# A six-layer fp32r transformer kernel on one core: joined matmuls of two widths, a mask in place of bias matmuls, and a reordered attention pipeline

## The chip, the cores and the metric

The kernel runs on one core of one Trainium2 chip. Its time is device microseconds (us) of that core for one execution; lower is better. The engines are PE (TensorE, matmuls), DVE (VectorE), ACT (ScalarE), POOL (GpSimd) and SP (SyncE, which issues DMA transfers). Each engine runs its own list of instructions in order, and the lists meet through semaphores.

## The reference

256 tokens of width 1024 in fp32 pass through two blocks. The first is a token mixer (8 heads of forgetting attention, 8 heads of banded attention) and a convolutional feed-forward layer; the second is a layer of retention with latent attention (MLA) and a layer of block-sparse attention (MoBA, 16 heads). Each ends in a residual and a layer norm. What matters here:

```python
def forgetting_attention(q, k, v, log_f):
    cum = jnp.cumsum(log_f.astype(jnp.float32), axis=-1)
    ...
        logits = jnp.einsum('bhqd,bhkd->bhqk', qb, k).astype(jnp.float32) * scale
        logits = logits + cb[..., :, None] - cum[..., None, :]
        ...
        logits = jnp.where(causal, logits, -jnp.inf)
        p = jax.nn.softmax(logits, axis=-1)

def conv_ffn(x, w_up, conv_w, conv_b, w_down):
    u = x @ w_up
    ...
    u = sum(u_pad[:, j:j + s, :] * conv_w[j] for j in range(CONV_WIDTH)) + conv_b
    value, gate = jnp.split(u, 2, axis=-1)
    return (value * jax.nn.gelu(gate)) @ w_down
```

## The kernel before

**Projections.** Every operand of a projection is held as two parts, hi and lo (hi is the value rounded to the fp32r type, lo the rest), and a product is the sum of three matmuls, hi by hi, hi by lo and lo by hi (`three`, lines 821 to 825). Weights arrive in 236 pieces of 128x1024 (512 KB each) in a buffer `raw`; ACT writes `w_hi` (`split_hi`, L1117) and DVE writes `w_lo` (`split_lo`, L1283) into a ring of six. Projections are cut into chunks (`chunks`); a chunk has a kind, a number of pieces and a place in four PSUM banks (`acc` 0 to 3). Kind F makes two tiles of 128 features by 256 tokens side by side in one bank: the weights stand still and the tokens move, 256 columns a matmul, 8 steps of the inner dimension. The feed-forward layer's up projection is 22 such pairs of tiles (value and gate). Two of them (`up01`) are made otherwise; `up2` to `up21` are kind F, one bank each.

**Convolution.** After the last matmul of `up j`, ACT makes the middle tap (`taps`, L1125) from PSUM, DVE adds the other two (`convolve`, L1326, four instructions), ACT makes the gelu, POOL multiplies, and ACT and DVE split the result (`h_split`, L1233 and L1447).

**Attention.** Heads go in pairs, `firsts` in `attention` being the first of each. Steps of a pair: `scores` on PE (L940, and for forgetting heads a second set, L949, four rows deep, that adds the cumulated gates through `cumA` and `cumB`); `soft` on DVE (adds the mask, takes the maximum, writes the probabilities' buffer `pr`); `exp` on ACT; `norm` on DVE; `pt` on PE (three 128x128 transposes a head, L959); a copy to `ptb` on ACT; `pv` on PE (the value products, L979); `yout` and `ylo`, which leave the result as hi and lo parts. Scores use job banks 0 and 1, transposes 2 and 3, value products 3 (banks 4 to 7 of `acc`). Layer one has 8 pairs (4 forgetting, 4 banded), layer two 4, layer three 8.

**Order.** `plan` writes one list of steps, `ORDER`, from which every engine takes its own. `run` emits a chunk's matmuls in halves of a piece; after each half, groups of attention steps from `pending` are emitted at a given rate (`background`), and splits run four pieces ahead. So an attention step sits on PE between projection matmuls. The last projection of each layer (`out1`, `down`, `out2`, `out3`, kind B) is normed by `norm_first`, `norm_half` and `norm_last`.

## Time and profile before

| | |
|---|---|
| median of 3 runs | 767.89 us (767.82 to 768.12) |
| the profiled execution | 768.47 us, of which the span from first to last instruction is 766.7 |
| mean granted TensorE clock | 0.996 of full speed |
| PE busy | 752.5 us, 98% |
| PE weight loads busy | 659.6 us, 86% |
| DVE busy | 528.8 us, 69% |
| ACT busy | 382.5 us, 50% |
| POOL busy | 36.8 us, 5% |
| DMA | 130.62 MB, mean 170 GB/s |

Matmuls are pipelined: one of 256 columns shows a duration of 0.28 us and the next starts 0.12 us after it. What a matmul takes of PE is the distance from its start to the next start, and that is how PE's rows are read here. For DVE and ACT the distance between starts is likewise a little less than the duration shown.

### The profile page before, as it was taken

The page shows a single profiled execution, that of the slowest core. Times are in us where ns is not written, and L with a number is a line of the kernel's source. Part 1 is how long each engine was busy: PE and PEld are TensorE (multiplying, and loading weights), DVE is VectorE, ACT ScalarE, POOL GpSimd, SP SyncE. Part 2 cuts the span into 40 slices and gives each one's busy share as a digit, 9 for nine tenths or more (in the row PEclk, how much of TensorE's full clock was granted, in tenths as well). Part 3 has the DMA queues.
Part 4 walks back from the last instruction along what each step waited for, and adds up shares of the span by engine and source line. Part 5 has one row for each costly group of instructions (what it writes and reads, how often), then busy time and mean ns, then how long its engine had stood idle before and what let it go on. Part 6 is the DMA issues. An engine that isn't in the chain of part 4 may idle for free.

```text
span 766.7 us, 12680 instructions
## 1 busy us (share of the span) xinstructions
PE 752.5 (98%) x4838; PEld 659.6 (86%) x4838; DVE 528.8 (69%) x940; ACT 382.5 (50%) x629; POOL 36.8 (5%) x50
## 2 busy tenths in 40 slices
PE   8999999999999999999999999999999999999995
PEld 8897777899999988799899777987788879988964
DVE  4654758697788854857686566965574587977766
ACT  5655763575655654156554444433443434565450
POOL 0000000021111200100000000000000010000001
PEclk9999999999999999999999999999999999999998
DMA  8852345456655685265536334553576617446402
GB/s 304 316 192 89 114 155 199 165 162 190 188 183 165 212 295 194 69 221 192 165 109 196 126 133 138 161 185 129 185 264 200 221 52 233 136 133 196 162 2 82
DMA packets 37580, 130.62 MB, mean 170 GB/s; under 512 B 4304, under 2 KB 4688, under 8 KB 37392
## 3 DMA queue, kind: packets, MB, share of 16 engines
q1 hardware_dynamic: 36144, 125.09, 49.2%
q0 software_dynamic: 1232, 4.46, 1.9%
q8 instruction: 39, 0.64, 0.3%
q10 hardware_dynamic: 144, 0.26, 0.1%
q14 instruction: 21, 0.17, 0.1%
HBM read 128.74 MB, written 1.05 MB: 169 GB/s over the span
## 4 chain that ended last, share of the span: by engine, by line
PE 95%; DVE 3%; issue 1%; DMA 1%; ACT 0%; DVEq 0%; SPq 0%
PE acc L823 28%; PE acc L825 27%; PE acc L824 27%; PE acc L940 2%; PE acc L959 2%; PE acc L979 2%; PE acc L998 1%; PE acc L938 1%; PE acc L1011 1%; PE acc L946 1%; DMA res<-in_x 1%; PE acc L972 0%; PE acc L1022 0%; PE acc L1037 0%; PE acc L1035 0%
## 5 line engine op out<-in xcount | busy, mean ns | idle before, releaser
L1283 DVE TENSOR_TENSOR w_lo<-raw,w_hi 128x1024 fp32r<-128x1024 f32 (+1 forms) x223 | 260.8, 1197 | 70.1 <-ACT w_hi L1117 69.3
L1117 ACT ACTIVATE w_hi<-raw 128x1024 fp32r<-128x1024 f32 (+1 forms) x223 | 224.4, 1034 | 88.8 <-PE acc L825 77.6
L823 PE MATMUL acc<-X_hi,w_hi 128*128 128x256 f32 x848 | 243.0, 287 | 0.6 <-DVE w_lo L1558 0.6
L824 PE MATMUL acc<-X_lo,w_hi 128*128 128x256 f32 x848 | 239.8, 283 | 0.0
L825 PE MATMUL acc<-X_hi,w_lo 128*128 128x256 f32 x848 | 239.8, 283 | 0.0
L823 PEld LDWEIGHTS acc<-X_hi,w_hi 128*128 128x128 f32 x848 | 162.5, 192 | 6.3 <-issue 5.1
L824 PEld LDWEIGHTS acc<-X_lo,w_hi 128*128 128x128 f32 x848 | 162.6, 192 | 0.5 <-issue 0.2
L825 PEld LDWEIGHTS acc<-X_hi,w_lo 128*128 128x128 f32 x848 | 162.5, 192 | 0.0
L823 PE MATMUL acc<-w_hi,S_hi 128*128 128x512 f32 x256 | 101.7, 397 | 1.3 <-DVE gate L1346 1.3
L824 PE MATMUL acc<-w_lo,S_hi 128*128 128x512 f32 x256 | 99.8, 390 | 0.0
L825 PE MATMUL acc<-w_hi,S_lo 128*128 128x512 f32 x256 | 99.7, 390 | 0.0
L823 PE MATMUL acc<-w_hi,X_hi 128*128 128x512 f32 (+1 forms) x192 | 74.4, 388 | 0.9 <-DVE w_lo L1283 0.9
L825 PE MATMUL acc<-w_hi,X_lo 128*128 128x512 f32 (+1 forms) x192 | 71.6, 373 | 0.0
L824 PE MATMUL acc<-w_lo,X_hi 128*128 128x512 f32 (+1 forms) x192 | 71.4, 372 | 0.0
L823 PEld LDWEIGHTS acc<-w_hi,S_hi 128*128 128x128 f32 x256 | 48.1, 188 | 13.0 <-issue 1.8
L825 PEld LDWEIGHTS acc<-w_hi,S_lo 128*128 128x128 f32 x256 | 48.1, 188 | 10.1
L824 PEld LDWEIGHTS acc<-w_lo,S_hi 128*128 128x128 f32 x256 | 48.1, 188 | 9.6 <-issue 0.2
L1326 DVE SCALAR_TENSOR_TENSOR v<-acc,cvp,v 128x255 f32<-128x255 f32 (+1 forms) x88 | 38.3, 477 | 20.9 <-ACT v L1125 20.1
L823 PEld LDWEIGHTS acc<-w_hi,X_hi 128*128 128x128 f32 x192 | 36.2, 189 | 9.4 <-issue 3.9
L1125 ACT ACTIVATE v<-acc,cvp 128x256 f32<-128x256 f32 x44 | 22.3, 561 | 42.6 <-PE acc L825 38.4
L825 PEld LDWEIGHTS acc<-w_hi,X_lo 128*128 128x128 f32 x192 | 36.2, 188 | 6.6
L824 PEld LDWEIGHTS acc<-w_lo,X_hi 128*128 128x128 f32 x192 | 36.3, 189 | 6.0 <-issue 0.5
(165 smaller groups left out, 795.7 us busy)
## 6 DMA issues: line engine op xcount, KB each, us to landing
raw<-in_w SPq DMA_DIRECT2D x225, 512.0 KB, 4.3
raw<-in_w SPq DMA_DIRECT2D x11, 256.0 KB, 3.1
gate<-in_ln_gain POOLq DMA_DIRECT2D x4, 512.0 KB, 5.2
gate<-in_ln_bias POOLq DMA_DIRECT2D x4, 512.0 KB, 5.7
res<-in_x SPq DMA_DIRECT2D x4, 256.0 KB, 4.2
gate<-in_bias SPq DMA_DIRECT2D x1, 1024.0 KB, 10.3
out<-res SPq DMA_DIRECT2D x4, 256.0 KB, 2.0
decay<-in_decay SPq DMA_DIRECT2D x1, 512.0 KB, 6.1
```

What stands on the lines that cost most here:

```text
L823: nc.tensor.matmul(out, a_hi, b_hi, start=start, stop=False)
L824: nc.tensor.matmul(out, a_hi, b_lo, start=False, stop=False)
L825: return nc.tensor.matmul(out, a_lo, b_hi, start=False, stop=stop)
L938: nc.tensor.matmul(dst, qT[s][:, h, q], kT[s][:, h, 0:nk], start=True, stop=False)
L940: last[i] = nc.tensor.matmul(dst, qT[s][rows, h // 2, q], kT[s][rows, h // 2, 0:nk], start=True, stop=kind != "fox")
L946: last[i] = nc.tensor.matmul(dst, qpeT[rows, h // 2, q], kpeT[rows, 0, 0:nk], start=False, stop=True)
L959: last = nc.tensor.transpose(job[:, 2 + j % 2, b * P:(b + 1) * P], pr[:, j % 2, b * P:(b + 1) * P], ident)
L979: last = nc.tensor.matmul(job[i * HD:(i + 1) * HD, 3, q0:q0 + n], vv[s][:, tt, v], ptb[:, (j + i) % 2, b0:b0 + n], start=tt == 0, stop=tt ...
L1117: nc.scalar.activation(home(u, "hi")[:, 0:n], raw[:, u % RAW, 0:n], ACT.Copy).then_inc(hi_done, 1)
L1125: return [nc.scalar.activation(conv[j % 2][:, i, :], up[:, i * S:(i + 1) * S], ACT.Identity, scale=cvp[:, 2, i, j:j + 1], bias=cvp[:, 3, i ...
L1283: nc.vector.tensor_tensor(home(u, "lo")[:, 0:n], raw[:, u % RAW, 0:n], home(u, "hi")[:, 0:n].bitcast(F32), ALU.subtract).then_inc(lo_done, 1)
L1326: last = nc.vector.scalar_tensor_tensor(o, up[:, i * S:i * S + S - lag], cvp[:, 2 - lag, i, j:j + 1], o, ALU.mult, ALU.add)
```

## The change

Six things are changed together.

1. `up2` to `up21` become kind W. The tokens' hi and lo parts now lie side by side (`X`, 512 columns for each step of the inner dimension), and one matmul of 512 columns with `w_hi` takes the place of two of 256; one of 256 with `w_lo` stays. A tile then fills a whole bank, its second half holding what comes of the lo part, and a chunk takes two banks. ACT copies the two second halves to `rtmp` and DVE adds the first halves to them; taps and convolution read `rtmp` and are put into the next chunk.
2. Forgetting heads: the matmuls of L949 are gone. POOL writes the cumulated gates (8 rows of 256) to DRAM and reads them back for all partitions; DVE adds the causal mask once (`fox_mask`), and `soft` adds the head's tile in place of the causal constant. (The term that belongs to the query falls out of the softmax.) DVE's work on the gates leaves `evac` of `f` and becomes the step `forgotten`, three halves later.
3. `attention` for layers one and three: `pv` of a pair stands directly behind the scores of the pair after the next, and `pt` stands alone in the middle of the round. For that a second set of probabilities (`spare`) lies where MLA's rotary parts lie, and `pr` and `spare` take turns.
4. `out3` starts in banks 2 and 3 instead of 0 and 1, and takes both its first pieces' first token tiles before their second.
5. The second half of the first weight piece is loaded after two of four pieces of `x`, and split after two of the four transposes.
6. The buffers for all this (`X`, `peT`).

```diff
@@ chunks @@
-        add(f"up{j}", "F", 2, "X", k8, "dve", ("conv", j),
+        add(f"up{j}", "W", 2, "X", k8, "dve", ("conv", j),
...
-    add("out3", "B", 8, "S", k8, "dve", ("norm", 3), ("w_out_odd", k8, None))
+    add("out3", "B", 8, "S", k8, "dve", ("norm", 3), ("w_out_odd", k8, None), at=2)
@@ plan @@
+        if of != "L2":
+            for i, e in enumerate(firsts):
+                p, o = (firsts[i - 1] if i else None), (firsts[i - 2] if i > 1 else None)
+                s0, s1, s2, s3 = [("scores", e)], [("exp", e), ("soft", e + 1)], [("exp", e + 1), ("norm", e)], [("norm", e + 1)]
+                if o is not None:
+                    s0.append(("pv", o))
+                    s1 = [("yout", o)] + s1 + ([("ylo", o)] if of == "L1" else [])
+                    s3 += [("ylo", o)] if of == "L3" else []
+                if p is not None:
+                    s2 += [("pt", p), ("pt", p + 1)]
+                s0.append(("soft", e))
...
+                pending.extend(zip(need, (s0, s1, s2, s3), gives))
+            o, p = firsts[-2:]
+            pending.append(({JOBS[o]["v"]}, [("pv", o), ("pt", p)], set()))
+            pending.append((gates(o), [("yout", o), ("ylo", o), ("pt", p + 1)], done(o)))
+            pending.append(({JOBS[p]["v"]}, [("pv", p)], set()))
+            pending.append((gates(p), [("yout", p)], set()))
+            pending.append((set(), [("ylo", p)], done(p)))
+            return
...
-    split_to(1)
+        if i == 1:
+            split_to(1)
...
-        run(name, 0)
+        run(name, 0, inside={(1, 1): [("forgotten",)]} if name == "kA0" else {})
...
-            run(f"up{j}", 0, tail=first if j == 2 else ())
+            run(f"up{j}", 0, tail=first if j == 2 else (),
+                inside={(0, 1): [("taps", j - 1)], (1, 0): [("conv", j - 1)]} if j > 2 else {})
...
-    run("out3", 1, lambda i: {f"L3y{i}"})
+    run("out3", 1, lambda i: {f"L3y{i}"}, early=2)
@@ PE @@
+                elif kind == "W":
+                    wait_operand(step, ch, [("X", tt, part) for tt in range(NT)])
+                    for k in range(4 * part, 4 * part + 4):
+                        w = slice(k * P, (k + 1) * P)
+                        nc.tensor.matmul(acc[:, b0 + i, :], wh[:, w], X[:, k, :, :], start=k == 0, stop=False)
+                        last = nc.tensor.matmul(acc[:, b0 + i, 0:S], wl[:, w], X_hi[:, k, :], start=False, stop=k == KT - 1)
...
-                        elif kind == "fox":
-                            r = slice(cum_row(h), cum_row(h) + 4)
-                            last[i] = nc.tensor.matmul(dst, cumA[r, h // 4, q], cumB[r, h // 4, 0:nk], start=False, stop=True)
@@ ACT @@
-                    last = taps(j, acc[:, b0, :])[1]
-                    last.then_inc(tap_act, 1)
+                    if j >= 4:
+                        act.wait_ge(conv_done, j - 1)
+                    nc.scalar.activation(rtmp[:, j % 2, :].rearrange("p (i s) -> p i s", i=2), acc[:, b0:b0 + 2, S:2 * S], ACT.Copy)\
+                        .then_inc(half_copied, 1)
...
+            def up_taps(j):
+                act.wait_ge(evac_dve, CH[BY[f"up{j}"]]["count"])
+                taps(j, rtmp[:, j % 2, :])[1].then_inc(tap_act, 1)
@@ DVE @@
-                    for g in range(2):
-                        for o, name in ((cumA, "cumA"), (cumB, "cumB")):
-                            k = const(name)
-                            last = nc.vector.tensor_scalar(o[:, g, :], fox[:, 0, :], k[:, g:g + 1], k[:, 2 + g:3 + g],
-                                                           ALU.mult, ALU.add)
-                    last.then_inc(evac_dve, 1)
+                    nc.vector.tensor_scalar(fox[:, 0, :], acc[:, b0, 0:S], bforget, None, ALU.add).then_inc(evac_dve, 1)
                 elif kind == "conv":
-                    convolve(e[1], acc[:, b0, :]).then_inc(evac_dve, 1)
+                    both = rtmp[:, e[1] % 2, :].rearrange("p (i s) -> p i s", i=2)
+                    dve.wait_ge(half_copied, e[1] - 1)
+                    nc.vector.tensor_tensor(both, both, acc[:, b0:b0 + 2, 0:S], ALU.add).then_inc(evac_dve, 1)
...
+            def fox_mask():
+
+                dve.wait_ge(cum_out, 16 * 2)
+                dve.wait_ge(const_in, 16)
+                tri = const("causal")[:, 0:P].unsqueeze(1).to_broadcast([P, 4, P])
+                for i in range(2):
+                    nc.vector.tensor_tensor(corner[:, 4 * i:4 * i + 4, :], forgot[i][:, :, 0:P], tri, ALU.add)
+                    last = nc.vector.tensor_tensor(forgot[i][:, :, P:S], forgot[i][:, :, P:S], tri, ALU.add)
+                link(last)
...
-                if j >= 2:
+                if jb["kind"] == "mla" or j in (24, 25):
                     dve.wait_ge(pt_ready, j - 1)
+                elif j >= 4:
+                    dve.wait_ge(pt_ready, j - 3)
+                x = probs(j)
...
+                elif jb["kind"] == "fox":
+                    first, rest = corner[:, jb["h"], :], forgot[jb["h"] // 4][:, jb["h"] % 4, :]
@@ POOL @@
+                    elif e[0] == "forget":
+                        pool.wait_ge(cum_ready, 1)
+                        pool.dma_start(cum_dram, fox[0:8, 2, :]).then_inc(cum_done, 16)
+                        pool.wait_ge(cum_done, 16)
+                        for i in range(2):
+                            pool.dma_start(forgot[i], cum_dram[4 * i:4 * i + 4, :].partition_broadcast(P)).then_inc(cum_out, 16)
@@ SP @@
+                        if (tt, q) == (0, 1):
+                            sp.dma_start(raw[:, 0, 512:1024], t["w"][0, :, 512:1024]).then_inc(landed[0], 16)
```

How instructions move, at three places. First PE in layer one, around the scores of the third pair of heads (forgetting heads 4 and 5). Before, L959 are the transposes of the second pair, L940 and L949 the scores of the third, L979 the value products of the second:

```order
380 L959 MATMUL acc<-cst,pr 128x128 x6
381 L940 MATMUL acc<-kT,qT 128x128 x2
382 L949 MATMUL acc<-rot 128x128 x2
383 L940 MATMUL acc<-kT,qT 128x256 x2
384 L949 MATMUL acc<-rot 128x256 x2
385 L979 MATMUL acc<-ptb,v 64x256 x2
386 L979 MATMUL acc<-ptb,v 64x128 x2
```

In the changed kernel L979 are scores, L1015 value products, L995 transposes:

```order
374 L979 MATMUL acc<-kT,qT 128x128 x2
375 L979 MATMUL acc<-kT,qT 128x256 x2
376 L1015 MATMUL acc<-ptb,v 64x256 x2
377 L1015 MATMUL acc<-ptb,v 64x128 x2
...
384 L995 MATMUL acc<-cst,peT 128x128 x6
```

The four-row matmuls are gone, the value products (now of the first pair) follow the scores, and the transposes (of the second pair, read from the spare set) come after the next projection matmuls. In this pair value products followed the scores before too; in the others projection matmuls stood between.

Then PE in the up projection, where one step of the inner dimension is three rows before and two in the changed kernel:

```order
708 L823 MATMUL acc<-X_hi,w_hi 128x256
709 L824 MATMUL acc<-X_lo,w_hi 128x256
710 L825 MATMUL acc<-X_hi,w_lo 128x256
```

```order
701 L908 MATMUL acc<-X,w_hi 128x512
702 L909 MATMUL acc<-X,w_lo 128x256
```

And DVE in the same stage, one chunk before (L1326 is the convolution, L1447 the split of `h`, L1283 the weight splits):

```order
184 L1326 SCALAR_TENSOR_TENSOR v<-acc,cvp,v 128x255 x2
185 L1326 SCALAR_TENSOR_TENSOR v<-acc,cvp,v 128x254 x2
186 L1447 TENSOR_TENSOR S_lo<-v,S_hi 128x256
187 L1283 TENSOR_TENSOR w_lo<-raw,w_hi 128x1024 x2
```

and one chunk of the changed kernel:

```order
191 L1418 TENSOR_TENSOR rtmp<-rtmp,acc 128x512
192 L1504 TENSOR_TENSOR S_lo<-v,S_hi 128x256
193 L1325 TENSOR_TENSOR w_lo<-raw,w_hi 128x1024
194 L1368 SCALAR_TENSOR_TENSOR v<-rtmp,cvp,v 128x255 x2
195 L1368 SCALAR_TENSOR_TENSOR v<-rtmp,cvp,v 128x254 x2
196 L1325 TENSOR_TENSOR w_lo<-raw,w_hi 128x1024
```

DVE has one instruction more, the convolution is that of the chunk before, and it stands between the two weight splits.

## Rows read from the trace of the kernel before

**Rows 1.** The page: busy time, share of the span, instructions.

```profile
PE 752.5 (98%) x4838; PEld 659.6 (86%) x4838; DVE 528.8 (69%) x940; ACT 382.5 (50%) x629; POOL 36.8 (5%) x50
```

**Rows 2.** Timeline of PE, up projection: start, duration, instruction.

```profile
240.06 0.28 PE L823 MATMUL acc<-X_hi,w_hi 128*128 128x256 f32 x1
...
240.42 0.28 PE L823 MATMUL acc<-X_hi,w_hi 128*128 128x256 f32 x1
```

**Rows 3.** Timeline of PE, down projection, matmuls of 512 columns.

```profile
300.00 0.39 PE L823 MATMUL acc<-w_hi,S_hi 128*128 128x512 f32 x1
...
300.68 0.39 PE L823 MATMUL acc<-w_hi,S_hi 128*128 128x512 f32 x1
```

**Rows 4.** Timeline of PE, the first pair's scores (forgetting heads).

```profile
48.74 0.49 PE L940 MATMUL acc<-kT,qT 64*128 64x128 f32 x4
...
50.22 0.70 PE L949 MATMUL acc<-rot 4*128 4x256 f32 x4
50.85 0.39 PE L823 MATMUL acc<-X_hi,w_hi 128*128 128x256 f32 x1
```

**Rows 5.** Timeline of PE, the first scores of layer three.

```profile
651.30 0.93 PE L940 MATMUL acc<-kT,qT 64*128 64x128 f32 x8
652.16 0.38 PE L823 MATMUL acc<-X_hi,w_hi 128*128 128x256 f32 x1
```

**Rows 6.** Timeline of PE: transposes of three pairs in layer one.

```profile
55.27 1.18 PE L959 MATMUL acc<-cst,pr 128*128 128x128 f32 x6
...
65.32 0.82 PE L959 MATMUL acc<-cst,pr 128*128 128x128 f32 x6
...
73.23 1.06 PE L959 MATMUL acc<-cst,pr 128*128 128x128 f32 x6
```

**Rows 7.** Timeline of PE: scores and value products without, then with matmuls between.

```profile
67.54 0.70 PE L949 MATMUL acc<-rot 4*128 4x256 f32 x4
68.17 0.87 PE L979 MATMUL acc<-ptb,v 128*64 128x256 f32 x8
...
83.20 0.50 PE L823 MATMUL acc<-w_hi,X_hi 128*128 128x512 f32 x1
83.54 0.40 PE L824 MATMUL acc<-w_lo,X_hi 128*128 128x512 f32 x1
...
84.48 0.39 PE L825 MATMUL acc<-w_hi,X_lo 128*128 128x512 f32 x1
84.80 0.87 PE L979 MATMUL acc<-ptb,v 128*64 128x256 f32 x8
```

**Rows 8.** Timeline of PE at the start: idle time and its releaser in brackets.

```profile
10.58 0.39 PE L823 MATMUL acc<-X_hi,w_hi 128*128 128x256 f32 x1 [0.59 <-DVE w_lo L1558]
24.74 0.47 PE L823 MATMUL acc<-w_hi,X_hi 128*128 128x512 f32 x1 [0.94 <-DVE w_lo L1283]
```

**Rows 9.** Timeline of DVE at the start, the last step of the gates.

```profile
21.97 1.38 DVE L1383 TENSOR_SCALAR rot<-rtmp,cst 128x256 f32<-128x256 f32 x4
```

**Rows 10.** Timeline of PE, the first matmul of `out3`.

```profile
730.07 0.50 PE L823 MATMUL acc<-w_hi,S_hi 128*128 128x512 f32 x1 [1.33 <-DVE gate L1346]
```

**Rows 11.** Timeline of DVE, one chunk of the up projection.

```profile
203.51 1.78 DVE L1326 SCALAR_TENSOR_TENSOR v<-acc,cvp,v 128x255 f32<-128x255 f32 x4 [1.37 <-ACT v L1125]
205.21 0.41 DVE L1447 TENSOR_TENSOR S_lo<-v,S_hi 128x256 fp32r<-128x256 f32 x1
...
209.27 1.78 DVE L1326 SCALAR_TENSOR_TENSOR v<-acc,cvp,v 128x255 f32<-128x255 f32 x4 [1.38 <-ACT v L1125]
```

**Rows 12.** Groups by line and shape, whole span: busy us, mean ns.

```profile
L1311 DVE TENSOR_TENSOR qT<-acc,tab 128x512 f32<-128x512 f32 x8 | 5.4, 678 | 0.0
...
L1366 DVE SCALAR_TENSOR_TENSOR rot<-rot,small,pr 128x256 f32<-128x256 f32 x4 | 1.7, 478 | 1.1 <-POOL small L1605 1.1
```

**Rows 13.** The same view of ACT.

```profile
L1156 ACT ACTIVATE kT<-acc 128x512 f32<-128x512 f32 x3 | 1.8, 591 | 6.1 <-PE acc L825 6.1
```

**Rows 14.** DMA issues by line: size and median us to landing.

```profile
gate<-in_ln_gain POOLq DMA_DIRECT2D x4, 512.0 KB, 5.2
```

More of the change, by code:

```diff
@@ L376, in attention @@
                 steps[3].append(("ylo", p))
-            of = "" if p is None else "L1" if p < 16 else "L2" if p < 24 else "L3"
-            gives = set() if p is None else {f"{of}y{JOBS[x]['tile']}" for x in (p, p + 1)}
+            gives = set() if p is None else done(p)
             for k in range(4):
@@ L749, in place, with probs @@
             return job[:, TJ[n]["bank"], :]
+        def probs(j):
+            return spare[:, j % 2, :] if JOBS[j]["kind"] != "mla" and j // 2 % 2 else pr[:, j % 2, :]
         def bank_free(eng, step):
@@ L1254, in _ @@
                     yout(step[1])
+                elif step[0] == "taps":
+                    up_taps(step[1])
                 elif step[0] == "gelu":
@@ L1565, in _ @@
                     evac(step[1])
+                elif step[0] == "forgotten":
+                    forgotten()
                 elif step[0] == "bias":
+                    fox_mask()
                     rel_bias()
```

106 lines of the change are left out of this document (54 added, 52 removed).

## The prediction

> **What bounds the kernel now.** I read the page first: PE is busy for 98% of the span [rows 1], at a mean granted clock of 0.996. So time is gained only where PE has fewer or shorter steps, or where it waits. A matmul's duration hides its neighbours, so I then read PE's timeline by distances between starts. In the up projection three matmuls of 256 columns take 240.42 - 240.06 = 0.36 us, 0.120 each [rows 2]; in the down projection three of 512 take 0.68, 0.2267 each [rows 3]. The difference, 0.1067 us for 256 more columns, is the columns' own time, and either kind carries 0.0133 us beyond it. Last I looked for every place where the distance is longer. The waits are few: 0.59 and 0.94 us at the start [rows 8] and 1.33 before `out3` [rows 10]; the rest is the short interludes of attention between projection matmuls.
>
> **The change, part by part.**
>
> *Joined matmuls.* One step of the inner dimension goes from 3 x 0.120 = 0.360 to 0.2267 + 0.120 = 0.3467 us [rows 2, 3]. There are 8 steps in each of 2 tiles of 20 chunks, 320: 320 x 0.0133 = 4.3 us. That assumes that DVE and ACT keep up with a chunk that takes PE 16 x 0.3467 = 5.55 us instead of 5.76. DVE's cycle is 5.76 us, of which it idles 1.38, so it works 4.38 [rows 11]. It gets the addition of 512 elements from PSUM; the nearest row is 678 ns [rows 12], of which some 0.08 overlaps the next instruction, as with the convolution (1.78 us long, but 1.70 to the next start [rows 11]). So 4.38 + 0.60 = 4.98, 0.57 below 5.55. The convolution now reads SBUF; an operation of that kind with all operands in SBUF has 478 ns [rows 12], and four of it in 1.78 us [rows 11] are 0.44 apart, so I price the move at nothing. ACT gets a copy of 512 (591 ns [rows 13]) and is half busy [rows 1]. Order matters too: DVE's addition waits for ACT's copy, which waits for the chunk's last matmul, but what is queued behind it (the split of `h`, a weight split) is not wanted by PE for four pieces, that is two chunks or 11 us. The two banks of a chunk are wanted again when the next chunk ends, 5.5 us later; the copy and the addition need about 0.6 + 0.7 us plus the semaphores. Only at the first chunks, where DVE is behind with the tiles of `up01`, do I see the margin shrink, to less than 1 us, and I take off 0.3 us for it (bounds 0 and 1).
>
> The Trainium skill, page "TensorE: Matmul & The Clock Gate", section "Back-to-back issue gap", gives a gap of N/2.4 plus 2.5 ns to a warm matmul. By it one matmul fewer would save 2.5 ns, and this part would give 320 x 2.5 ns = 0.8 us in place of 4.3. The trace disagrees with it at both widths (120 and 226.7 ns against 109 and 216), and I go by the trace.
>
> *Forgetting heads.* The first pair's scores, alone between projection matmuls, take 50.85 - 48.74 = 2.11 us [rows 4]; a pair without the four-row matmuls takes 0.86 [rows 5]. Four pairs: 4 x 1.25 = 5.0 us. That is more than those matmuls' columns, since switching between the two kinds goes too. DVE's addition of the mask costs the same with a head's tile as with the constant. `fox_mask` adds four operations of 512 on DVE, about 2.4 us by the 0.60 above, ahead of the first scores, where DVE has finished its splits; if all of it came late it would push the first scores' chain by 2.4 us, which two halves of projection matmuls cover. The gates travel by DRAM: a write and two reads of 512 KB, on a queue where a transfer of that size lands in 5.2 us [rows 14]. The gates are ready at about 24 (21.97 + 1.38 before [rows 9]); with 3 us for the write, 1 to issue and 8 to land among the weights' transfers they are back at 36. The masks are wanted some 4 us ahead of the first scores (48.74 [rows 4]), at about 44. Cost nothing; each us beyond 44 would cost one.
>
> *Transposes.* In the second and fourth pairs PE's transposes take 1.18 and 1.06 us against 0.82 in the third [rows 6], because they come before the probabilities of the second head are done. They now come two halves later in the chain: 0.36 + 0.24 = 0.6 us.
>
> *Seams.* The first projection matmul after scores is followed at 83.54 - 83.20 = 0.34 us, 0.11 more than 0.227, and the value products start 84.80 - 84.48 = 0.32 after the last matmul, 0.09 more [rows 7]. Leaving fp32 and entering it again costs 0.20. Where value products directly follow scores, the distance is 68.17 - 67.54 = 0.63 [rows 7], the same as from the last scores to a projection matmul, 50.85 - 50.22 [rows 4], so the 0.20 is not paid. The new order has this seam in the third to eighth pair of both layers, 12 times, and it was there once before: 11 x 0.20 = 2.2 us. Between transposes and scores there was no such saving to lose: both are priced here by their own rows. Bounds: 0 (if taking the transposes out adds a switch) and 3.
>
> *Gates on DVE.* PE waits 0.94 us at 24.74 for a weight split [rows 8] that stands behind DVE's work on the gates, of which the last part alone is 1.38 us long [rows 9]. Now that split stands ahead of it: 0.9 us, and the four small operations become one.
>
> *`out3`.* Its first matmul waits 1.33 us for the gate of `mgt11` [rows 10], which holds bank 1. From banks 2 and 3 on, held by chunks long done, it can start, and bank 1 comes two pieces later, 2.7 us of matmuls (12 x 0.2267): 1.3 us. At the end of layer three the last pair's value products get one group of six matmuls as cover (1.4 us) instead of three; behind them lie three operations of 256 elements (0.41 each [rows 11]), about 1.3 with semaphores. I price that at nothing, bounds 0 and 0.5.
>
> *Start.* The second half of the first weights is loaded and split earlier; it can take at most the 0.59 us of [rows 8], and the last two pieces of `x` are 256 KB later. I take 0.3 (bounds 0 and 0.6).
>
> **Sum.** 4.3 - 0.3 + 5.0 + 0.6 + 2.2 + 0.9 + 1.3 + 0.3 = 14.3 us. The profiled execution took 768.47 us, 1.77 of it outside the span of 766.7; that frame stays, so it would be 754.2. The median of the runs shown is 0.58 below the profiled one, so I forecast 767.89 - 14.3 = 753.6 us. What ends the kernel, DVE's norm after `out3`, hangs on PE's matmuls of that chunk and moves with them.
>
> **The rivals.**
>
> *The joined matmuls give nothing.* Either the 0.0133 us goes with the columns read and not with the instruction, or DVE, with 0.57 us to spare, does not fit its waits in. For it: 90% load on an engine in strict order, and the `angles` operations come on top in four chunks. Against it: the same 0.0133 at two widths [rows 2, 3], and work four pieces ahead. The time is 753.6 + 4.0 = 757.6. The page's figure stands here as well, as a cost per instruction that is mostly not saved, at 757.1. Chance 0.13, of it 0.04 for the page's rule.
>
> *The attention part gives only the bias matmuls.* Seams and transposes give nothing (2.8 us), or the new order brings waits of that size: `pt` of the second head and `pv` share bank 3, and DVE carries the masks late. Against it: the distances in [rows 7]. Time 755.6 to 757. Chance 0.14.
>
> *Slower: DVE sets the pace of the up projection.* If waits for ACT's copy and taps cannot be filled with splits, a chunk lasts 4.98 us and the waits. PE then waits for banks, because a chunk has two banks of four where it had one. Each 0.1 us over 5.55 costs 20 x 0.1 = 2 us; the kernel is slower from 5.55 + 14.3 / 20 = 6.27 us on, which needs 1.3 us of unfilled waits per chunk. At 6.5 the time would be 753.6 + 19 = 772.6. Against it: a split stands between the addition and the convolution, just where a wait for the taps would be. Chance 0.05, of it 0.02 within 0.2% and 0.03 slower.
>
> *More than forecast.* The start gives all of 0.6, other seams (value products before transposes at the layers' ends) count, nothing is lost at the first chunks: below 751.8. Chance 0.04.
>
> **How the numbers follow.** The forecast case, 751.8 to 755.5, has 0.64. With the attention rival it is 0.78; taking in most of the first rival gives 751.6 to 757.7. Faster by over 0.2% (1.5 us, about what a measurement of this kernel tells from no change) holds all cases but the slower one: 0.95; within it 0.02; slower 0.03.
>
> **What would show it.** In the up projection PE's starts should be 0.227 and 0.120 us apart in turn and a chunk 5.55 us, with DVE idle about half a us per chunk; a longer chunk with an idle time released by the addition says the first or third rival. Scores and value products together should take about 0.86 + 0.80 us in every pair, with no idle time released by DVE at the transposes, and the waits at 10.6, 24.7 and at `out3` should be gone or short. A wait of DVE for the DMA that brings the gates back would be a cost I put at nothing.

## The result, and the profile after

The changed kernel takes 759.13 us in the median of 4 runs (756.82 to 759.28), the kernel before on the same chip 767.86 (767.68 to 768.12): a ratio of 0.988, 95% interval 0.986 to 0.990. That is 8.7 us or 1.1% less, where 14.3 us were forecast; the median lies above the range. The profiled execution is the fastest of the four, 756.82 us with a span of 755.0, and it is 11.65 us shorter than the profiled one of before. The miss of 5.5 us has three parts: 14.3 - 11.65 = 2.65 us that are in the trace, 2.3 us by which the median exceeds the traced run (the three others are at 759.06 to 759.28, their mean granted clock is 0.994, its own 0.996), and 0.6 because before it was the other way round and the traced run was slower than the median.

The page of the changed kernel, part 1 and two groups of part 5 (what stood at L823 to L825 is L858 to L860 now; the joined matmuls are L908 and L909):

```profile
span 755.0 us, 12053 instructions
PE 741.0 (98%) x4486; PEld 638.5 (85%) x4486; DVE 544.6 (72%) x961; ACT 394.1 (52%) x649; POOL 41.6 (6%) x53
...
L908 PE MATMUL acc<-X,w_hi 128*128 128x512 f32 x320 | 111.2, 392 | 0.0
...
L909 PE MATMUL acc<-X,w_lo 128*128 128x256 f32 x320 | 89.6, 280 | 0.0
```

PE is still busy for 98% of the span, so the gain has to be found in distances between starts again. In the up projection PE's timeline (start, duration) reads:

```profile
240.30 0.39 PE L908 MATMUL acc<-X,w_hi 128*128 128x512 f32 x1
240.53 0.28 PE L909 MATMUL acc<-X,w_lo 128*128 128x256 f32 x1
240.65 0.39 PE L908 MATMUL acc<-X,w_hi 128*128 128x512 f32 x1
```

A step of the inner dimension is 0.35 us, where it was 0.36 [rows 2]. DVE's timeline has one whole chunk from split to split:

```profile
202.83 1.23 DVE L1325 TENSOR_TENSOR w_lo<-raw,w_hi 128x1024 fp32r<-128x1024 f32 x1 [0.19 <-ACT w_hi L1153]
203.97 1.79 DVE L1368 SCALAR_TENSOR_TENSOR v<-rtmp,cvp,v 128x255 f32<-128x255 f32 x4
205.67 1.22 DVE L1325 TENSOR_TENSOR w_lo<-raw,w_hi 128x1024 fp32r<-128x1024 f32 x1
206.89 0.69 DVE L1418 TENSOR_TENSOR rtmp<-rtmp,acc 128x512 f32<-128x512 f32 x1
207.49 0.70 DVE L1504 TENSOR_TENSOR S_lo<-v,S_hi 128x256 fp32r<-128x256 f32 x1
208.38 1.23 DVE L1325 TENSOR_TENSOR w_lo<-raw,w_hi 128x1024 fp32r<-128x1024 f32 x1 [0.18 <-ACT w_hi L1153]
```

The cycle is 208.38 - 202.83 = 5.55 us, PE's pace. The addition takes 0.60 to the next start and the convolution 1.70, both as priced. DVE is shown idle for only 0.18 us of it, less than the half us foreseen. Part of the rest is the split of `h` (L1504): it takes 0.70 us in the seven chunks where POOL's multiplication runs beside it for 0.42 us, as here (POOL's starts at 207.17 and takes 0.74), and 0.42 in the chunks where the two hardly overlap; before the change the two did not meet in these chunks. From 155 to 180 us, where DVE catches up, a chunk takes it 4.91 us with no idle time, near the 4.98 of the estimate. PE never waits for DVE here.

The waits at the start of the second half (10.58), at 24.74 [rows 8] and before `out3` [rows 10] are gone. Behind the first 6 us, PE's timeline marks only these two waits:

```profile
7.66 0.55 PE L1034 MATMUL acc<-cst,res 128*128 128x128 f32 x3 [0.50 <-DMA res<-in_x]
...
108.54 0.52 PE L995 MATMUL acc<-cst,peT 128*128 128x128 f32 x3 [1.92 <-DVE S_lo L1499]
```

**By stage.** From PE's timeline I take the starts of the first projection matmul, of the first scores, of the transposes of `x` between the layers, and of the last matmul. The feed-forward layer and layer three are counted from the last of the transposes ahead of them, layer one and layer two up to the first; the two stretches of 9.0 us left out between them are the same before and after. All stages are us.

| stage | before | after | gain | forecast |
|---|---|---|---|---|
| to the first half's first projection matmul | 8.33 | 8.95 | -0.62 | start 0.3 and gates 0.9, to the first scores |
| from there to the first scores | 40.41 | 38.72 | 1.69 | |
| layer one's attention, from the first scores | 80.17 | 75.88 | 4.29 | 5.0 + 0.6 + 5 seams 1.0 |
| feed-forward layer | 180.49 | 176.59 | 3.90 | 4.3 - 0.3 |
| layer two | 299.22 | 299.28 | -0.06 | 0 |
| layer three, to the last matmul | 130.72 | 128.24 | 2.48 | 6 seams 1.2, `out3` 1.3 |

The feed-forward layer and layer three came out as forecast. Layer one gives 2.3 us less. The place is the wait at 108.54: the transposes of head 15, the last of the layer, wait 1.92 us for DVE's L1499, which is `ylo` of the pair before (heads 12 and 13). PE, ACT and DVE around it:

```profile
104.69 0.55 PE L995 MATMUL acc<-cst,peT 128*128 128x128 f32 x3
...
106.23 0.39 PE L860 MATMUL acc<-w_hi,S_lo 128*128 128x512 f32 x1
108.54 0.52 PE L995 MATMUL acc<-cst,peT 128*128 128x128 f32 x3 [1.92 <-DVE S_lo L1499]
...
105.28 0.49 ACT L1252 ACTIVATE ptb<-acc 128x384 f32<-128x384 f32 x1 [2.11 <-PE acc L995]
105.66 2.00 ACT L1153 ACTIVATE w_hi<-raw 128x1024 fp32r<-128x1024 f32 x2
107.56 0.38 ACT L1261 ACTIVATE S_hi<-acc 128x256 fp32r<-128x256 f32 x1
...
106.75 1.23 DVE L1325 TENSOR_TENSOR w_lo<-raw,w_hi 128x1024 fp32r<-128x1024 f32 x1 [2.71 <-ACT w_hi L1153]
107.97 0.42 DVE L1499 TENSOR_TENSOR S_lo<-acc,S_hi 128x256 fp32r<-128x256 f32 x1
```

Read from the end: L1499 (107.97) waits for L1261, which is `yout` (107.56). That one needs only the value products of 103.89, done by 104.8. But on ACT it stands behind two weight splits (2.00 us), and on DVE L1499 stands behind two `w_lo` splits, of which the second waits for ACT. The list of steps that `plan` writes for the changed kernel has there:

```
pv 12
pt 14
mm out1.2 p(0,)
split_hi 31
split_hi 32
split_lo 30
split_lo 31
yout 12
ylo 12
pt 15
```

`pt 15` writes bank 3. `pv 12` has left its result there, and it is free only after `ylo 12`. A second, smaller case of the same is the third pair's transposes (start 70.29), which add 0.99 us between projection matmuls where the others add 0.66.

### The profile page after: what moved, and what is told of

It is laid out like the page before. It is cut to its first block, busy times and chain, and to the rows that moved or that the text cites. A ratio compares the mean times of both kernels' runs of the same rounds, so it can differ in the third digit from the quotient of the medians.

```text
span 755.0 us, 12053 instructions
## 1 busy us (share of the span) xinstructions
PE 741.0 (98%) x4486; PEld 638.5 (85%) x4486; DVE 544.6 (72%) x961; ACT 394.1 (52%) x649; POOL 41.6 (6%) x53
## 4 chain that ended last, share of the span: by engine, by line
PE 97%; DVE 1%; DMA 1%; issue 0%; SPq 0%; DVEq 0%; ACT 0%; ACTq 0%
PE acc L858 24%; PE acc L860 23%; PE acc L859 23%; PE acc L908 10%; PE acc L909 5%; PE acc L995 2%; PE acc L979 2%; PE acc L1015 2%; PE acc L1034 1%; PE acc L977 1%; PE acc L1047 1%; DMA res<-in_x 1%; PE acc L985 1%; PE acc L1008 0%; PE acc L1058 0%; PE acc L1071 0%
## 5 line engine op out<-in xcount | busy, mean ns | idle before, releaser
L858 PE MATMUL acc<-X,w_hi 128*128 128x256 f32 x528 | 152.2, 288 | 0.1
L860 PE MATMUL acc<-X,w_lo 128*128 128x256 f32 x528 | 149.3, 283 | 0.0
L859 PE MATMUL acc<-X,w_hi 128*128 128x256 f32 x528 | 149.3, 283 | 0.0
L908 PE MATMUL acc<-X,w_hi 128*128 128x512 f32 x320 | 111.2, 392 | 0.0
L858 PEld LDWEIGHTS acc<-X,w_hi 128*128 128x128 f32 x528 | 101.1, 191 | 3.7 <-issue 3.0
L858 PE MATMUL acc<-w_hi,S_hi 128*128 128x512 f32 x256 | 101.9, 398 | 0.0
L859 PEld LDWEIGHTS acc<-X,w_hi 128*128 128x128 f32 x528 | 101.2, 192 | 0.4 <-issue 0.2
L860 PEld LDWEIGHTS acc<-X,w_lo 128*128 128x128 f32 x528 | 101.1, 192 | 0.0
L860 PE MATMUL acc<-w_hi,S_lo 128*128 128x512 f32 x256 | 99.8, 390 | 0.0
L909 PE MATMUL acc<-X,w_lo 128*128 128x256 f32 x320 | 89.6, 280 | 0.0
L858 PE MATMUL acc<-w_hi,X 128*128 128x512 f32 (+1 forms) x192 | 74.2, 386 | 0.0
L860 PE MATMUL acc<-w_hi,X 128*128 128x512 f32 (+1 forms) x192 | 71.6, 373 | 0.0
L859 PE MATMUL acc<-w_lo,X 128*128 128x512 f32 (+1 forms) x192 | 71.5, 372 | 0.0
L908 PEld LDWEIGHTS acc<-X,w_hi 128*128 128x128 f32 x320 | 59.9, 187 | 13.2
L909 PEld LDWEIGHTS acc<-X,w_lo 128*128 128x128 f32 x320 | 60.5, 189 | 0.0
L858 PEld LDWEIGHTS acc<-w_hi,S_hi 128*128 128x128 f32 x256 | 48.1, 188 | 11.1 <-issue 1.4
L860 PEld LDWEIGHTS acc<-w_hi,S_lo 128*128 128x128 f32 x256 | 48.1, 188 | 10.1
L858 PEld LDWEIGHTS acc<-w_hi,X 128*128 128x128 f32 x192 | 36.2, 189 | 7.3 <-issue 1.8
```

Of the source, the lines that this page charges most:

```text
L858: nc.tensor.matmul(out, a_hi, b_hi, start=start, stop=False)
L859: nc.tensor.matmul(out, a_hi, b_lo, start=False, stop=False)
L860: return nc.tensor.matmul(out, a_lo, b_hi, start=False, stop=stop)
L908: nc.tensor.matmul(acc[:, b0 + i, :], wh[:, w], X[:, k, :, :], start=k == 0, stop=False)
L909: last = nc.tensor.matmul(acc[:, b0 + i, 0:S], wl[:, w], X_hi[:, k, :], start=False, stop=k == KT - 1)
```

## The experiments

Theory A: bank 3 costs about 2 us at the layer's end because two weight splits stand ahead of `yout` and `ylo`, and an idle PE of about 2 us is what lets the clock fall in some runs, which is the rest. Theory B, the rival: the joined matmuls or the new order give less than priced in most runs, and the wait is only where it shows. The medians of before beside which the following were timed are 768.14 us (first four), 768.19 (next four) and 768.02 (last three). In line numbers of other kernels the same lines stand a few lines further down.

**1. `yout` and `ylo` ahead of the splits.**

```diff
-            pending.append(({JOBS[o]["v"]}, [("pv", o), ("pt", p)], set()))
-            pending.append((gates(o), [("yout", o), ("ylo", o), ("pt", p + 1)], done(o)))
+            if of == "L1":
+                pending.append(({JOBS[o]["v"]}, [("pv", o), ("pt", p), ("yout", o), ("ylo", o)], done(o)))
+                pending.append((set(), [("pt", p + 1)], set()))
...
```

> The changed kernel, but at the end of layer one the last pair but one gets its yout and ylo steps directly behind its value products, ahead of the weight splits, instead of behind them. Theory A (the second head's transposes wait at 108.5 us for bank 3, because ylo stands behind two weight splits on ACT, and the 2 us of idle PE also let the clock fall in most runs): the profiled span falls by 2.0 us to about 753.0, and the times of all runs lie together at about 754.8, 4.3 below the changed kernel's median of 759.1. Rival B (the wait is real, but the two levels of the runs come from the changed start of the kernel): the span falls by 2.0 and the times stay on two levels, about 754.8 and 757.2. Rival C (the wait only hides another one behind it, such as the copy of the probabilities): the span falls by less than 0.5.

Measured: 755.76 us (ratio 0.984, 0.983 to 0.985; one disturbed run of 4174 us is left out). Layer one's attention takes 73.99 us in the place of 75.88. PE's timeline at the place:

```profile
106.90 0.39 PE L864 MATMUL acc<-w_hi,S_lo 128*128 128x512 f32 x1
107.32 0.52 PE L999 MATMUL acc<-cst,peT 128*128 128x128 f32 x3
107.60 0.48 PE L862 MATMUL acc<-w_hi,S_hi 128*128 128x512 f32 x1
```

The wait is gone but for some 0.2 us: these transposes add 0.56 us between projection matmuls, where those at the end of layer three add 0.34. All four runs have a clock of 0.996 or 0.997. The profiled span is 753.9 us and not the 753.0 expected, because the first scores start at 48.37 us in this trace and at 47.67 in that of after. The median is 3.4 us under the first comparison's 759.13, and 2.0 under that of experiment 8, the same kernel on this chip: 1.6 under its runs at a clock of 0.997, and 3.2 under its run at 0.994. So the wait itself and something that goes with the clock are both gone.

**2. The wait filled.** The wait stays as long as it is, but PE does four matmuls of 256 columns in it (fp32, no part of the output; the trace records each as two).

```diff
             def pt(step):
                 j = step[1]
+                if j == 15:
+                    pe.wait_ge(max_done, 16)
+                    for _ in range(4):
+                        nc.tensor.matmul(job[:, 0, 0:256], kT[0][:, 0, 0:P], kT[0][:, 0, :], start=True, stop=True)
```

> The changed kernel with four more matmuls of 256 columns in fp32 on PE ahead of the transposes of head 15, so that PE works through most of the 1.9 us that it idles there; they write a bank that nothing reads. Theory A (the idle time lets the clock fall in most runs): the span stays at about 755.0 (up to 0.3 more), and all runs take about 756.8, with the mean clock 0.996. Rival B (the start decides): most runs stay at 759.1 with clock 0.994.

Measured: 757.61 us (757.08 to 757.80; 0.986, 0.985 to 0.988), the clock 0.997 in all four. The trace:

```profile
107.25 1.89 PE L995 MATMUL acc<-kT 128*128 128x256 f32 x8
109.33 0.52 PE L999 MATMUL acc<-cst,peT 128*128 128x128 f32 x3 [0.18 <-DVE S_lo L1503]
```

Layer one takes 75.85 us, the same as after, since the order of the splits is the same. (The median is 0.8 us above the 756.8 expected, and so is the start of the first scores above that of after, 48.49 to 47.67.) So the time of the wait is kept and only the idleness taken away, and the runs at the lower clock are gone with it: the four agree with the runs at 0.997 of experiment 8 (757.36 and 757.42).

**3. The old order of attention,** with all the rest of the change: `if of != "L2":` becomes `if False:`.

> The changed kernel with attention's old order in layers one and three (transposes ahead of the scores, value products a half later), the mask, the joined matmuls, out3 and the start kept. My account of the reorder (11 seams at 0.20 us gained, 2.1 us lost at head 15's transposes and 0.3 at those of the third pair): the span is about 755.0 - 2.4 + 2.2 = 754.8, and by theory A all runs lie near 756.6 on one level. If the seams gain nothing, the span is 752.6. By rival B the runs lie on two levels, most near 759.

Measured: 758.25 us (758.11 to 758.56; 0.987, 0.986 to 0.989). That is 0.5 us above the changed kernel in experiment 8 and 0.9 below it in the first comparison: the new order had little more than paid for its own wait. (By stage the trace of after is 0.6 us longer in layer one and 1.4 shorter in layer three. I had expected the old order 0.2 us shorter in all; it is 0.8 longer.) Against experiment 1, which has the new order without the wait, it is 2.5 us slower. By stage that is 75.27 - 73.99 = 1.28 us in layer one and 129.65 - 128.24 = 1.41 in layer three, 2.7 together. The forecast for the order was 2.2 for seams and 0.6 for transposes.

**4. The up projection as before,** narrow matmuls, one bank a chunk, taps and convolution from PSUM (of the edit, the part that says it).

```diff
-        add(f"up{j}", "W", 2, "X", k8, "dve", ("conv", j),
+        add(f"up{j}", "F", 2, "X", k8, "dve", ("conv", j),
...
-            run(f"up{j}", 0, tail=first if j == 2 else (),
-                inside={(0, 1): [("taps", j - 1)], (1, 0): [("conv", j - 1)]} if j > 2 else {})
+            run(f"up{j}", 0, tail=first if j == 2 else ())
```

> The changed kernel with the up projection as before: kind F, one bank a chunk, three matmuls of 256 columns a step, taps and convolution from PSUM. Forecast 320 x 0.0133 us less what the first chunks lose: the stage from the layer's first transposes to those of the next layer takes 3.9 to 4.3 us longer, the span 758.9 to 759.3. If the addition on DVE had slowed the stage, less than that.

Measured: 761.74 us (761.16 to 763.15; 0.992, 0.991 to 0.994). The feed-forward layer takes 180.49 us again, to the hundredth what it took before, and no other stage moves; the joined matmuls are worth 3.90 us there. Between the medians of experiments 4 and 8 lie 4.0 us. Its starts are 0.120 apart as in [rows 2].

**5. The bias matmuls back.** The four-row matmuls are put back in the forgetting heads' scores, adding zeros, while DVE's way of adding the gates stays.

```diff
                             last[i] = nc.tensor.matmul(dst, qT[s][rows, h // 2, q], kT[s][rows, h // 2, 0:nk],
-                                                       start=True, stop=True)
+                                                       start=True, stop=kind != "fox")
...
+                        elif kind == "fox":
+                            pe.wait_ge(const_in, 16)
+                            r = slice(64 * (h % 2) + 32 * (h // 2 % 2), 64 * (h % 2) + 32 * (h // 2 % 2) + 4)
+                            zero, mask = const("causal")[:, P:2 * P], const("causal")[:, P:3 * P]
+                            last[i] = nc.tensor.matmul(dst, zero[r, :], mask[r, 0:nk], start=False, stop=True)
```

> The changed kernel with the four-row matmuls put back behind the scores of the forgetting heads; they add zeros, so the result is that of the mask. My term: 4 x 1.25 = 5.0 us more in layer one, of which the waits of the transposes can take some away. If switching between kinds does not count, only the matmuls' own 4 x 1.05 = 4.2.

Measured: 762.85 us (762.16 to 764.88; 0.994, 0.993 to 0.995). Layer one's attention takes 80.90 - 75.88 = 5.02 us more; the forecast was 4 x 1.25 = 5.0. The other stages stay.

**6. The start as before,** on top of experiment 1.

```diff
-        if i == 1:
-            split_to(1)
+    split_to(1)
...
                     for tt, q in ((0, 0), (1, 0), (0, 1), (1, 1)):
-                        if (tt, q) == (0, 1):
-                            sp.dma_start(raw[:, 0, 512:1024], t["w"][0, :, 512:1024]).then_inc(landed[0], 16)
...
+                    sp.dma_start(raw[:, 0, 512:1024], t["w"][0, :, 512:1024]).then_inc(landed[0], 16)
```

> The kernel of e1_early_yout (changed, with the two steps ahead of the splits) with the start as before: the second half of the first weights loaded after all of x and split after the four transposes. I had given the new start 0.3 us; the traces so far show the second half of the first chunk at 10.7 to 11.1 us against 10.6 before. Theory now: the new start gives nothing, the last pieces of x come later, and this kernel is 0 to 0.4 us faster than e1_early_yout. Rival: it is 0.3 us slower.

Measured: 755.00 us (754.71 to 755.87; 0.983, 0.982 to 0.985), 0.8 us under experiment 1. The two traces, experiment 6 first:

```profile
7.21 0.66 PE L1036 MATMUL acc<-cst,res 128*128 128x128 f32 x4 [0.35 <-DMA res<-in_x]
...
8.49 0.36 PE L860 MATMUL acc<-X,w_hi 128*128 128x256 f32 x1
...
10.75 0.39 PE L860 MATMUL acc<-X,w_hi 128*128 128x256 f32 x1 [0.58 <-DVE w_lo L1617]
```

The wait of 0.58 us for the weight split is back, and the kernel is no slower, by its median faster. With the changed start the wait for the third piece of `x` is 1.14 us in experiment 1, 1.29 in experiment 8 and 0.50 in the first trace, and the first projection matmul starts at 8.95 to 9.77 us in the eight traces that have it, against 8.10 to 8.49 in those with the old start, but for experiment 11 (9.07). The first scores come 0.58 us earlier than in experiment 1. I had allowed 0 to 0.4 us; by this pair of kernels the change of the start loses 0.6 (traces) to 0.8 us (medians). How large the loss is, the runs do not settle: the first scores start at 47.67 to 48.50 us in the eight traces with the changed start (mean 48.24) and at 47.47, 47.79 and 48.33 in experiments 9, 6 and 11 with the old one (mean 47.86), and the two ranges overlap. No run shows a gain.

**7. The wait made longer.** Two additional operations of 1024 elements on DVE ahead of `ylo 12` (on a buffer that nobody reads then).

```diff
             def ylo(j):
...
+                if j == 12:
+                    for _ in range(2):
+                        link(nc.vector.tensor_tensor(rtmp[:, :, :], ryb[:, :, :], ryb[:, :, :], ALU.subtract))
```

> The changed kernel with two more operations of 1.2 us each on DVE ahead of ylo of the pair before the last in layer one (they write a buffer that nothing reads any more), so that PE idles there for about 4.3 us instead of 1.9. Theory A: the clock falls in all runs; besides the 2.4 us of longer wait every run pays 2 us or more for matmuls at 1.2 GHz behind it, so all lie at 761.5 or above with a mean clock of 0.994 or less, and the rows behind the wait show matmuls of twice the distance. Rival B (the levels come from the start): the runs lie on two levels, 2.4 us above those of the changed kernel.

Measured: 762.49 us (761.68 to 763.23; 0.993, 0.992 to 0.994), with the clock at 0.994 or 0.992 in all five runs. PE's wait:

```profile
111.80 0.70 PE L995 MATMUL acc<-cst,peT 128*128 128x128 f32 x3 [4.36 <-DVE S_lo L1502]
112.15 0.78 PE L858 MATMUL acc<-w_hi,S_hi 128*128 128x512 f32 x1
```

and by windows (us, busy time of PE, PEld, DVE, ACT and POOL, granted clock, DMA share, GB/s):

```profile
108.00:110.00 2.00, 0.00 (x0) 0.00 (x0) 1.97 (x3) 0.76 (x2) 0.00 (x0) 1.00 0.43 133
110.00:112.00 2.00, 0.20 (x2) 0.23 (x3) 1.97 (x3) 0.00 (x0) 0.00 (x0) 1.00 0.68 236
112.00:114.00 2.00, 2.00 (x7) 1.62 (x6) 0.79 (x1) 1.47 (x3) 0.00 (x0) 0.50 0.15 23
114.00:118.00 4.00, 4.00 (x20) 2.59 (x19) 3.32 (x4) 2.81 (x4) 0.00 (x0) 0.82 0.75 239
```

Layer one takes 79.86 us, 3.98 more than after: 4.36 - 1.92 = 2.44 of it is waiting, and 1.54 is matmuls at half clock. I had expected 2 us or more for these; the traced run has less, and the four others, at a clock of 0.992, are 0.6 to 1.6 us longer than it.

**8. The changed kernel again,** unaltered, to get a trace of a run at the lower clock.

> The changed kernel itself once more, so that it stands beside the others on one chip. Theory A (its wait of 1.9 us at head 15's transposes lets the clock fall in some runs and not in others): runs on two levels, about 757 with a mean clock of 0.996 to 0.997 and about 759.2 with 0.993 to 0.994.

Measured: 757.76 us (757.36 to 758.93; 0.986, 0.985 to 0.988). The traced run is the slowest of the four, 758.93 us at a clock of 0.994; two others have 0.997 (757.36 and 757.42) and one 0.996 (758.10). It has the very same wait, and then:

```profile
109.00 0.52 PE L995 MATMUL acc<-cst,peT 128*128 128x128 f32 x3 [1.92 <-DVE S_lo L1499]
109.28 0.47 PE L858 MATMUL acc<-w_hi,S_hi 128*128 128x512 f32 x1
...
110.06 0.58 PE L858 MATMUL acc<-w_hi,S_hi 128*128 128x512 f32 x1
110.44 0.63 PE L859 MATMUL acc<-w_lo,S_hi 128*128 128x512 f32 x1
110.86 0.63 PE L860 MATMUL acc<-w_hi,S_lo 128*128 128x512 f32 x1
...
113.50 0.41 PE L859 MATMUL acc<-w_lo,S_hi 128*128 128x512 f32 x1
```

```profile
108.00:110.00 2.00, 1.00 (x6) 0.94 (x7) 1.99 (x3) 0.84 (x4) 0.00 (x0) 1.00 0.31 76
110.00:112.00 2.00, 2.00 (x8) 1.02 (x9) 0.97 (x1) 1.95 (x3) 0.00 (x0) 0.53 0.80 270
112.00:114.00 2.00, 2.00 (x12) 1.29 (x9) 1.82 (x3) 0.98 (x2) 0.00 (x0) 0.62 0.64 234
```

At 110.1, one us after PE has taken up its work, a matmul of 512 columns becomes 0.63 us long and 0.42 apart, twice the columns' time, until 113.4. The windows show the granted clock at 0.53 and 0.62, so the 1.2 GHz level; the trace of after has 1.00 in the same windows. The Trainium skill, page "TensorE: Matmul & The Clock Gate", section "Wait — 56ns, not 53.3ns?", gives 426.7 ns from start to start for 512 columns on the cold array, and this trace agrees with its 0.42. Layer one takes 77.41 us here against 75.88, 1.53 more, and everything behind it is the same to 0.07.

**9. `out3` in its old banks** (on top of experiment 6).

```diff
-    add("out3", "B", 8, "S", k8, "dve", ("norm", 3), ("w_out_odd", k8, None), at=2)
+    add("out3", "B", 8, "S", k8, "dve", ("norm", 3), ("w_out_odd", k8, None))
...
-    run("out3", 1, lambda i: {f"L3y{i}"}, early=2)
+    run("out3", 1, lambda i: {f"L3y{i}"})
```

> The kernel of e6_start_old with out3 as before: from bank 0, without the first token tiles ahead. My term: PE waits 1.3 us again for the gate of mgt11, so layer three from its last transposes of x to the last matmul takes 1.3 us longer than the 128.23 of the other runs. Rival: with the transposes gone from ahead of the scores, the wait is shorter by part of it (0.7 us of cover lost or won), 0.6 to 2.0.

Measured: 755.73 us (755.36 to 756.03; 0.984, 0.983 to 0.985), 0.7 us more than experiment 6, which was timed on another chip. Layer three takes 128.82 - 128.23 = 0.59 us more. PE's first matmul of `out3`:

```profile
716.36 0.50 PE L860 MATMUL acc<-w_hi,S_hi 128*128 128x512 f32 x1 [0.53 <-DVE gate L1390]
```

The wait comes back with 0.53 us and not with the 1.33 of [rows 10], just below the lower bound of the rival (0.6).

**10. DVE's work on the gates back in its old place** (on top of experiment 6).

```diff
-        run(name, 0, inside={(1, 1): [("forgotten",)]} if name == "kA0" else {})
+        run(name, 0)
+        if name == "f":
+            emit(("forgotten",))
```

> The kernel of e6_start_old with the step forgotten directly behind the evacuation of f on DVE, ahead of the weight split that PE wants next. If only the place counts, PE waits again near 24 us, by about 0.9 us or a little less, since three of the four small operations are gone (1.38 us before, 0.29 now). Rival: the wait came from those operations, and it is now below 0.2 us.

Measured: 755.36 us (754.89 to 755.78; 0.983, 0.982 to 0.985), 0.4 more than experiment 6, hardly more than the comparison can tell. From the first projection matmul to the first scores it takes 47.95 - 8.10 = 39.85 us, where experiment 6 has 39.30. PE has one new wait, and none near 24:

```profile
12.40 0.39 PE L862 MATMUL acc<-X,w_hi 128*128 128x256 f32 x1 [0.34 <-DVE w_lo L1329]
```

This one is not of the gates' making: it is for the second weight piece, whose split on ACT waited 0.53 us for its loading. DVE's small operations on the gates behind ACT's, up to the next weight split, take 21.47 - 20.07 = 1.40 us here and 23.27 - 20.78 = 2.49 before. They also begin 0.7 us earlier here, since the bias of the gates landed earlier, but the 1.1 us saved are more than the wait by themselves. So the 0.94 us of [rows 8] went mainly with the operations themselves (four small ones became one), and their place gives little.

**11. `ylo` ahead of the exponentials in every round** (on top of experiment 6), so that bank 3 is free earlier for the third pair.

```diff
-                    s1 = [("yout", o)] + s1 + ([("ylo", o)] if of == "L1" else [])
+                    s1 = [("yout", o)] + ([("ylo", o)] if of == "L1" else []) + s1
```

> The kernel of e6_start_old with ylo directly behind yout in layer one, ahead of exp and of the second head's soft. Theory: the third pair's transposes, 0.99 us instead of 0.66 in the changed kernel, wait for bank 3, which ylo frees; then layer one is 0.3 us shorter, 73.7 instead of 74.0. Rival: soft of the second head now waits behind ylo, and other transposes wait in its place: 74.0 or longer.

Measured: 754.96 us (754.61 to 757.06; 0.983, 0.982 to 0.984), not to be told from experiment 6. Layer one's attention takes 73.65 us, 0.37 less than in experiment 6, and the third pair's transposes are like the others:

```profile
70.94 0.82 PE L997 MATMUL acc<-cst,pr 128*128 128x128 f32 x6
71.52 0.48 PE L860 MATMUL acc<-w_hi,X 128*128 128x512 f32 x1
```

The traced run is the slowest of its five; its feed-forward layer takes 178.35 us where every other kernel with joined matmuls has 176.59. There each step of the inner dimension takes 0.3533 us (0.2333 and 0.12), from the first chunk to the last, where the others have 0.3467 (0.23 and 0.1167, by means of the starts from 165 to 240 us), at a granted clock of 1.00 and with no wait on PE. Half of the 0.0133 us a step that the joined matmuls give was lost in this run. The four other runs cannot have had it, by their times. I have no cause for it.

## Why the prediction was wrong, by its own steps

**Right, with their sizes.** The joined matmuls: 4.3 less 0.3 foreseen, 3.90 measured (experiment 4). The reason for the 0.3 was another one: no wait shows at the first chunks, and of the 0.37 between 320 x 0.0133 and the stage, about 0.2 are two seams in the down projection that are 0.1 us wider. So the 0.0133 us belongs to the instruction and goes with it, as the trace of before had it. The Trainium skill, page "TensorE: Matmul & The Clock Gate", section "Back-to-back issue gap", gives the 2.5 ns, by which it would have been 0.8 us, for an isolated warm matmul; for a stream with a weight load to each matmul it gives about 131 ns at 512 columns. The traces disagree with both: 3.90 us in the stage, and 226.7 ns a matmul [rows 3]. Bias matmuls: 5.0 foreseen, 5.02 measured (experiment 5). Seams: PE's timeline of after shows scores and value products together as

```profile
67.14 0.93 PE L979 MATMUL acc<-kT,qT 64*128 64x128 f32 x8
67.99 0.87 PE L1015 MATMUL acc<-ptb,v 128*64 128x256 f32 x8
68.80 0.50 PE L858 MATMUL acc<-w_hi,X 128*128 128x512 f32 x1
69.13 0.40 PE L859 MATMUL acc<-w_lo,X 128*128 128x512 f32 x1
```

The last projection matmul before them starts at 66.82; 69.13 - 66.82 less two matmuls of 0.2267 is 1.86 us. In experiment 3, apart, scores add 1.05 and value products 1.00; the joint saves the 0.20 that was priced. (Taking the transposes away from the scores costs nothing, as was said: together they add 1.71 in experiment 3's layer three, alone 0.66 and 1.04 in that of after.) (The text's "0.86 + 0.80 in every pair" as a sign was too low; it left one entry and exit out.) Gates and their DRAM trip: from the second half's first matmul to the first scores 48.74 - 10.58 = 38.16 before and 47.67 - 10.70 = 36.97 now, a gain of 1.19 for the 0.9 foreseen. Nothing waited for the DMA: the two reads are issued at 25.48 and 26.05 us and land 8.1 and 10.3 us later, at about 36 as estimated, and DVE begins `fox_mask` at 44.44.

**The step that failed** is the one on the seams, where the new order was costed only by what it joins, with "both are priced here by their own rows", and nothing was charged for the banks. That `pt` of the second head and `pv` share bank 3 stood in the rival "the attention part gives only the bias matmuls", at a chance of 0.14, and no place was looked for where it would bite. It bites at the end of layer one. The last group holds `yout`, `ylo` and `pt` together, and the planner writes the late weight splits ahead of a group: two on ACT (2.00 us) and two on DVE stand before the two short steps that free the bank. Inside the rounds there is more work between `pv` and the next `pt`, and it only costs 0.33 once. I had priced the end of layer three (at nothing, and rightly: no wait shows there, and in the list of steps only `split_lo 235`, the last split of all, stands ahead of `yout 36`), and never looked at the end of layer one, where the same steps meet weight splits.

**What it cost.** In the profiled execution: 2.1 us at the wait (the interlude of head 15's transposes adds 2.44 us, that of layer three 0.34; experiment 1 takes out 1.9 and leaves 0.2) and 0.33 at the third pair. In the median more: where the clock falls after it, another 1.5 us (experiment 8). Experiment 1 takes out the wait, experiment 2 only the idleness; together they show that both parts hang on this wait. Theory B falls: with the wait out, joined matmuls and order give what was priced. What is not settled is the whole of the 2.3 us between the traced run of after and its three others. 1.5 are the clock by experiment 8's trace; some may be the start, whose first projection matmul varies between 8.95 and 9.77 us, but those runs have no trace.

**Start: the sign was wrong.** The wait of 0.59 was taken away as said. But the last two pieces of `x`, 256 KB later, are what the transposes wait for, and these stand ahead of the first matmul: -0.12 in the profiled execution (10.58 before, 10.70 after, at the second half) and -0.4 to -0.8 by experiment 6 and the means of the traces. The text named the 256 KB and gave it no price.

**`out3`: the sum was right for half a reason.** 2.5 us were forecast for layer three and 2.48 measured. Of the 1.3 us of `out3`, its banks and order give only 0.59 under the new order of attention (experiment 9); 0.8 of the wait go with that order. Under the old one they give 130.72 - 129.65 = 1.07 (experiment 3 against before): its trace has no wait at `out3`, but the transposes ahead of the eighth pair's scores take longer,

```profile
726.02 1.13 PE L995 MATMUL acc<-cst,pr 128*128 128x128 f32 x6
727.09 0.93 PE L979 MATMUL acc<-kT,qT 64*128 64x128 f32 x8
```

1.07 us from start to start where the pairs before have 0.75. These 0.32 us are also what the order's 1.41 in layer three hold beyond six seams.

**Without the wait and with the old start** (experiment 6) the profiled execution takes 755.15 us, 13.3 less than before, of 14.3 foreseen: 0.95 to the first scores (1.2 foreseen), 6.15 in layer one (6.6), 3.91 (4.0), -0.1 and 2.49 (2.5). So of the miss of 5.5 us in the median, 2.1 are the wait, 1.5 the clock after it where it falls, 0.3 the third pair, and 0.4 or more the start, less 0.3 that the gates gave beyond their price; 0.6 are the place of before's traced run among its own. Some 0.8 stay open, of which the start may be a part. Experiment 6, with 755.00, is the kernel I would keep: 13.2 us or 1.7% under the one before.

## What to carry to other kernels

When steps are joined or moved in a software pipeline, list for every buffer that changes hands which step frees it, and read in the planned order what stands ahead of that step on its own engine, above all at the ends of a stage where there are fewer rounds to hide it. A short step that frees a bank (here 0.4 us on ACT and 0.4 on DVE) belongs ahead of work that is done in advance, such as weight splits. And a wait of PE can cost more than its length: if it cannot be removed, the four runs of experiment 2 show that filling it with matmuls that nobody reads keeps the clock.

## What the hardware showed that I had not expected

The same 1.92 us of idle PE lowered the clock in one traced run and not in another. Kernels with this wait (after and experiments 4, 5 and 8) had runs at a mean clock of 0.993 or 0.994 and runs at 0.996 to 0.998, 8 and 10 of 18; in experiments 4 and 5 too, the two runs at the lower clock are the slowest of their five. With 4.36 us of waiting all 5 runs were at 0.992 to 0.994. Of the kernels without it or with it filled (experiments 1, 3, 6, 9, 10 and 11, and experiment 2), and of the kernel before, no run was below 0.995. In experiment 8's trace the fall comes only one us after PE has resumed, when it is busy again, and lasts some 3.3 us; in experiment 7, behind the longer wait, the first whole window after it is at 0.50 already. By the windows PE was 1.00 of 2 us busy from 108 to 110, at a clock of 1.00, before it fell.
